# Two transformer-like blocks on one core: surplus tile spread over the last expert pack, combine and norms by token tile, second block's end reordered

## The chip, the cores and the metric

The kernel runs on one core of a Trainium2 chip. The metric is device time in microseconds of one launch, all weights read from HBM. The engines are TensorE (PE, with its weight loads as PEld), VectorE (DVE), ScalarE (ACT), GpSimd (POOL) and SyncE (SP, here the queue that issues nearly all transfers).

## What is computed

256 tokens of width 1024, in float32, pass through two blocks. Cut to what matters here:

```python
# end of the first block: hierarchical MoE, 32 experts, each token goes to 2 of them
h = h + sum_over_experts(combine[:, e] * (silu(xt @ w_gate[e]) * (xt @ w_up[e])) @ w_down[e])
x = rmsnorm(h, final_norm_g)                       # "first"
# second block
h = rms_norm(x, g_mix)                             # "mix2"
z = h @ w_in + b_in                                # 56 chunks of 128 columns
va, ga, xb, gb, sa, sb = split(z)
u = silu(layer_norm(causal_conv31(va * sigmoid(ga)), ln_g, ln_b));  y_a = u @ w_a_out
v = rg_lru(causal_conv4(xb));                      y_b = (v * gelu(gb)) @ w_b_out
x = x + (sigmoid(sa) * y_a + sigmoid(sb) * y_b) @ w_o
h = rms_norm(x, g_mlp)                             # "mlp2"
x = x + square(relu(h @ w_1)) @ w_2
return rms_norm(x, g_final)                        # "last"
```

An expert has a tile of 32 token slots. An expert with more tokens than that needs a surplus tile; `n_extra` counts them at run time, and with these inputs there is one.

## The kernel before, in words

All five engines run hand-written programs that meet at counting semaphores; each engine works strictly in program order. Dense products are float32 made of three faster passes: a matrix is kept as a rounded part ("hi", written by ScalarE) and the remainder ("rest", subtracted on VectorE or GpSimd), and `three_passes` (L1595 to L1597) multiplies hi by hi, hi by rest and rest by hi.

**Experts.** SP streams 6 MB for each expert (gate, up, down). `load_pair` (L465, L468) alternates two sets of three 2 MB slots: an expert's gate and up may be issued when the expert two before has finished its gate and up products (`gu_done`), its down when that one has finished down (`down_done`). Experts go in packs of four. Packs 1 to 6 are a loop, pack 7 is written out: TensorE does `expert_gate_up` (L1749) and `expert_down` (turn of the hidden rows L1756, products L1762) for experts 28 to 31, with the surplus tile between them under `pe.If(n_extra > 0)`: after expert 28's down come `over_gate_up(0)` (gather L1845, turn L1848, products L1749), then expert 29's gate and up, `over_down(0)`, expert 29's down, and `over_combine(0)` (L1868), which waits until VectorE has added the four results (L1355). Then come experts 30 and 31. `combine_pack` (L1775) multiplies the pack's weighted rows back to tokens in four parts, both token tiles of the first half of the columns and then both of the second; VectorE adds each to `X` (`add_pack`, L1247).

**Two norms.** After the last add, `moe_done` is set. VectorE writes HG = X * g_first (L1382), ScalarE sums the squares of X (L660) and of HG (L843); the root of the first norm and its reciprocal scale the sums for the second root (L1386, L1387, L848), then VectorE writes the normalised rows `HN` (L1391) and the new X (L1393). TensorE turns HN (L1588), VectorE applies the gain (L1031), ScalarE writes HT_hi (L676), VectorE HT_rest (L1040).

**In-projection.** 28 halves of 256 columns (1 MB each), in the order IN2_ORDER, four raw buffers in the slots that the experts' gate and up had. SP issues the first four after `down_done` of expert 30, later ones as buffers come free. ScalarE rounds each (`split_half`, L803), GpSimd subtracts (L600), except halves 16 to 18 and 22 to 25, which VectorE subtracts (L1403). TensorE makes two chunks from a half (`times_hT`), ScalarE takes them (L865). ScalarE's order is: take half n, then `split_half(n + 4)`. VectorE runs beside this: four pairs of the 31-tap convolution (L1411, L1418, L1425), six of the short one, the recurrence (L1462 to L1490) with one `rest_half` after each of its four groups.

**Layer norm.** Mean and variance over channels are products with a matrix of 1/1024 (`mean_ones`): `means()` (L1936) has 8 matmuls after the in-projection, `variances()` (L1942) 8 more after the third of the y_b products. **Out-projection.** Four halves of w_o, each for both token tiles (`o_ps`), then VectorE adds (L1547), the norm "mlp2" (L660, L663, L1016), turn, gain, hi, rest. `residual_first` (L1807) loads X into the four result banks by products with the identity. **MLP.** Two rounds of four w_1 blocks and four w_2 blocks of 2 MB. ScalarE rounds each (`split_mlp`, L963), VectorE subtracts (L1539). Inside a w_1 block ScalarE does four relus (L980), then `split_mlp` of a block four further on, then FT_hi (L983). **End.** When all of w_2 is used, VectorE copies four banks to X (L1573), ScalarE sums squares of both token tiles, one root, then L1576 writes the result, and SP stores it in two transfers (L553).

## Time and profile before

| | us |
|---|---|
| median of 3 runs | 1159.42 |
| lowest, highest | 1159.11, 1169.11 |
| the profiled execution | 1171.32 |
| its span on the core | 1169.5 |
| mean granted TensorE clock in it (1.0 is 2.4 GHz) | 0.891 |

The page gives for the span: PE busy 919.2 us (79%), PEld 745.3 (64%), DVE 497.5 (43%), ACT 369.0 (32%), POOL 203.5 (17%); 298 MB are read at a mean of 256 GB/s. Stamps below are microseconds from the start of the span. "Idle before <- X" is time in which the engine waited and what came last.

### The profile page before, as it was taken

The page shows a single profiled execution, that of the slowest core. Times are in us where ns is not written, and L with a number is a line of the kernel's source. Part 1 is how long each engine was busy: PE and PEld are TensorE (multiplying, and loading weights), DVE is VectorE, ACT ScalarE, POOL GpSimd, SP SyncE. Part 2 cuts the span into 40 slices and gives each one's busy share as a digit, 9 for nine tenths or more (in the row PEclk, how much of TensorE's full clock was granted, in tenths as well). Part 3 has the DMA queues.
Part 4 walks back from the last instruction along what each step waited for, and adds up shares of the span by engine and source line. Part 5 has one row for each costly group of instructions (what it writes and reads, how often), then busy time and mean ns, then how long its engine had stood idle before and what let it go on. Part 6 is the DMA issues. An engine that isn't in the chain of part 4 may idle for free.

```text
span 1169.5 us, 18121 instructions
## 1 busy us (share of the span) xinstructions
PE 919.2 (79%) x7868; PEld 745.3 (64%) x7868; DVE 497.5 (43%) x784; ACT 369.0 (32%) x508; POOL 203.5 (17%) x76
## 2 busy tenths in 40 slices
PE   4988486856666665657588489998999989999996
PEld 4977476524233333333254389778999988888985
DVE  5434623411212120202021649999973446453541
ACT  4452411110101010101011434456656443534330
POOL 1031400000000000000000688702139820000000
PEclk9997585977889787978797889999999998999998
DMA  9850370999999999999998445424556643354510
GB/s 356 256 220 1 128 304 1 392 421 421 424 422 424 421 421 421 422 421 421 422 421 370 146 149 179 144 73 144 167 173 235 217 148 140 145 215 163 197 72 36
DMA packets 94891, 299.79 MB, mean 256 GB/s; under 512 B 9165, under 2 KB 45565, under 8 KB 86653
## 3 DMA queue, kind: packets, MB, share of 16 engines
q1 hardware_dynamic: 94125, 297.95, 65.7%
q0 software_dynamic: 576, 1.18, 0.4%
q8 instruction: 34, 0.56, 0.2%
q14 instruction: 12, 0.10, 0.0%
q10 hardware_dynamic: 144, 0.00, 0.0%
HBM read 298.07 MB, written 1.05 MB: 256 GB/s over the span
## 4 chain that ended last, share of the span: by engine, by line
PE 53%; DMA 25%; DVE 14%; ACT 4%; issue 2%; SPq 1%; POOL 0%; DVEq 0%; ACTq 0%; POOLq 0%
DMA mem<-in_w_up 22%; PE PS L1595 12%; PE PS L1596 11%; PE PS L1597 11%; PE PS L1749 9%; DVE PS L1425 6%; PE PS L1762 3%; DMA mem<-in_w 2%; PE PS L1588 1%; PE PS L1737 1%; ACT mlp_hi L963 1%; DVE ring_rest L1403 1%; ACT mem L660 1%; DVE HN L1125 1%; DVE mem L1382 1%
## 5 line engine op out<-in xcount | busy, mean ns | idle before, releaser
L1749 PE MATMUL PS<-mem 128*32 128x256 f32 x2048 | 156.1, 472 | 111.4 <-DMA mem<-in_w_up 110.1
L1597 PE MATMUL PS<-HT_hi,ring_rest 128*128 128x256 f32 x768 | 218.8, 285 | 0.0
L600 POOL TENSOR_TENSOR ring_rest<-mem,z_hi 128x2048 fp32r<-128x2048 f32 x21 | 98.4, 4691 | 619.1 <-ACT z_hi L803 540.6
L1749 PEld LDWEIGHTS PS<-mem 128*32 128x32 f32 x2048 | 83.8, 135 | 185.0 <-issue 163.5
L1597 PEld LDWEIGHTS PS<-HT_hi,ring_rest 128*128 128x128 f32 x768 | 148.6, 193 | 0.0
L1595 PE MATMUL PS<-HT_hi,z_hi 128*128 128x256 f32 x448 | 129.2, 288 | 9.9 <-ACT mem L865 5.7
L1596 PE MATMUL PS<-HT_rest,z_hi 128*128 128x256 f32 x448 | 128.4, 287 | 0.0
L1234 DVE TENSOR_TENSOR mem<-mem,PS 128x128 f32<-128x128 f32 x32 | 9.2, 287 | 241.9 <-ACT mem L776 241.9
L1539 DVE TENSOR_TENSOR ring_rest<-mem,mlp_hi 128x4096 fp32r<-128x4096 f32 x16 | 70.6, 4425 | 82.4 <-ACT mlp_hi L963 82.4
L1595 PEld LDWEIGHTS PS<-HT_hi,z_hi 128*128 128x128 f32 x448 | 87.7, 196 | 11.9 <-ACT mem L865 6.1
L1425 DVE SCALAR_TENSOR_TENSOR PS<-mem,CAW,PS 128x256 f32<-128x256 f32 x232 | 91.2, 479 | 0.0
L1596 PEld LDWEIGHTS PS<-HT_rest,z_hi 128*128 128x128 f32 x448 | 87.6, 196 | 0.0
L776 ACT ACTIVATE mem<-PS 128x128 f32<-128x128 f32 x32 | 8.9, 278 | 239.8 <-PE PS L1749 239.8
L963 ACT ACTIVATE mlp_hi<-mem 128x4096 fp32r<-128x4096 f32 x16 | 57.8, 3624 | 81.6 <-DMA mem<-in_w 81.6
L1595 PE MATMUL PS<-HT_hi,mlp_hi 128*128 128x256 f32 x256 | 72.5, 283 | 4.2 <-ACT mem L980 4.2
L803 ACT ACTIVATE z_hi<-mem 128x2048 fp32r<-128x2048 f32 x28 | 53.5, 1914 | 68.2 <-DMA mem<-in_w_in 68.2
L1762 PE MATMUL PS<-mem 128*32 128x256 f32 x1024 | 63.0, 386 | 14.7 <-ACT mem L780 14.7
L1596 PE MATMUL PS<-HT_rest,mlp_hi 128*128 128x256 f32 x256 | 72.2, 282 | 0.0
L1239 DVE COPY mem<-PS 32x256 f32<-32x256 f32 x64 | 27.2, 424 | 71.5 <-PE PS L1762 70.8
L1762 PEld LDWEIGHTS PS<-mem 128*32 128x32 f32 x1024 | 36.5, 110 | 31.8 <-issue 20.6
L1588 PE MATMUL PS<-ident,HN 128*128 128x128 f32 x80 | 18.6, 424 | 43.9 <-DVE HN L1016 19.4
L1595 PEld LDWEIGHTS PS<-HT_hi,mlp_hi 128*128 128x128 f32 x256 | 48.6, 190 | 5.5 <-ACT mem L980 5.0
(322 smaller groups left out, 1887.7 us busy)
## 6 DMA issues: line engine op xcount, KB each, us to landing
mem<-in_w_gate SPq DMA_DIRECT2D x32, 2048.0 KB, 15.2
mem<-in_w_up SPq DMA_DIRECT2D x32, 2048.0 KB, 19.7
mem<-in_w_down SPq DMA_DIRECT2D x32, 2048.0 KB, 12.0
mem<-in_w SPq DMA_DIRECT2D x16, 2048.0 KB, 7.9
mem<-in_w_in SPq DMA_DIRECT2D x28, 1024.0 KB, 5.3
mem<-in_w_in SPq DMA_DIRECT2D x5, 2048.0 KB, 19.3
mem<-in_w_b_out SPq DMA_DIRECT2D x4, 1536.0 KB, 8.7
mem<-in_w_out SPq DMA_DIRECT2D x2, 2048.0 KB, 15.0
```

The costliest lines, as they stand in the source:

```text
L600: nc.gpsimd.tensor_tensor(z_rest(n), z_raw(n), z_hi(n).bitcast(F32), ALU.subtract).then_inc(z_rest_ready, 1)
L803: nc.scalar.activation(z_hi(n), z_raw(n), ACT.Copy).then_inc(z_hi_ready, 1)
L963: nc.scalar.activation(mlp_hi[n % 4][:, :], slot[late_slot[n % 4]], ACT.Copy).then_inc(mlp_hi_ready, 1)
L1239: ins = nc.vector.tensor_copy(Y[SLOTS * i:SLOTS * (i + 1), D_STRIP * j:D_STRIP * (j + 1)], PS[SLOTS * j:SLOTS * (j + 1), B_DOWN + i % 2, 0 ...
L1425: nc.vector.scalar_tensor_tensor(to, UP[:, ch, k:k + T], CAW[:, k * KC + ch:k * KC + ch + 1], acc[:, i, :], ALU.mult, ALU.add).then_inc(ta ...
L1539: nc.vector.tensor_tensor(ring_rest[late_slot[n % 4]][:, :], slot[late_slot[n % 4]], mlp_hi[n % 4][:, :].bitcast(F32), ALU.subtract).then_ ...
L1588: ins = nc.tensor.transpose(PS[:, 4 + n, k * P:(k + 1) * P], HN[:, tt, 4 * half + k, :], ident[:, :])
L1595: nc.tensor.matmul(dst, s_hi, m_hi, start=start and n == 0, stop=False, skip_group_check=True)
L1596: nc.tensor.matmul(dst, s_hi, m_rest, start=False, stop=False, skip_group_check=True)
L1597: ins = nc.tensor.matmul(dst, s_rest, m_hi, start=False, stop=stop and n == len(terms) - 1, skip_group_check=True)
L1749: ins = nc.tensor.matmul(PS[SLOTS * j:SLOTS * (j + 1), bank, 0:2 * F_STRIP].rearrange("p (w n) -> p w n", w=2), xg[:, k, :], w[:, :, k, F_ ...
L1762: ins = nc.tensor.matmul(PS[SLOTS * j:SLOTS * (j + 1), bank, 0:D_STRIP], hT[:, SLOTS * k:SLOTS * (k + 1)], w[:, k, D_STRIP * j:D_STRIP * ( ...
```

## The change

1. **Surplus tile.** Its parts move. TensorE: gather after expert 28's gate and up, gate and up after expert 29's, down after expert 29's down, combine after expert 30's gate and up; the wait for its adds moves to before expert 31's down. ScalarE's and VectorE's programs are cut accordingly. Surplus tiles from the second on, of which there are none here, come before expert 30's down.
2. **First loads of the in-projection** wait for the gate and up of expert 30 (not its down).
3. **Last combine by token tile**: both halves of tile 0, then of tile 1. Squares of a tile start when its own adds are done. `moe_done` goes.
4. **One root for both norms.** The second root takes the sum of squares of HG and, as bias, (eps/D * sum of squares of X + eps*eps), so that it waits for no first root; one root for each token tile. The first norm's own root and the new X come later (after HT_rest). GpSimd subtracts half 0 in four pieces and then waits for HG; half 1 goes to VectorE, ahead of the first convolution.
5. **First product in another order**: hi by hi and rest by hi for all k, and only then the passes that need HT_rest, also for the MLP. The first of the in-projection's rounds is written out.
6. **Layer norm**: VectorE sums the 8 chunks first (`tensor_reduce` of 2048 elements over a view with k innermost), so that one matmul stands in place of 8, for the mean and for the variance. The mean's goes before the last round of the in-projection; centring moves ahead of h_rest and the squares to half 25 in ScalarE's program.
7. **Out-projection** in the order WO_ORDER. X is turned as it is, unnormalised, by token tile (`turn_x3`), tile 0 before the last two steps. The norm of the MLP is applied at the end as the square of the reciprocal root (relu, squared, scales so). `residual_first` goes; the end does X = PSUM * r2 + X.
8. **MLP**: ScalarE does `split_mlp` after the second relu of the next block; both rounds are written out. The last w_2 block goes by result bank, token tile 0 first, and the end is done by token tile and half, with three stores.

```diff
-            sp.wait_ge(down_done, EXPERTS - 1)
+            sp.wait_ge(gu_done, EXPERTS - 1)
             for n in range(RAW):
                 load_z(n)
...
+            pool.wait_ge(z_hi_ready, 1)
+            for part in range(4):
+                at = slice(part * BLOCK, (part + 1) * BLOCK)
+                ins = nc.gpsimd.tensor_tensor(z_rest(0)[:, at], z_raw(0)[:, at], z_hi(0)[:, at].bitcast(F32), ALU.subtract)
+            ins.then_inc(z_rest_ready, 1)
+            pool.wait_ge(gained, TT)
...
+            pool.wait_ge(z_rest_ready, 2)
             for n in range(2, IN2_HALVES):
...
+            split_half(0)
             act.preload_act_table_set(SQRT_SET)
+            for tt in range(TT):
+                act.wait_ge(comb_free, 4 * (PACKS - 1) + 2 + 2 * tt + 2)
+                nc.scalar.activation(turned_rows[:, tt, :], X[:, tt, :], ACT.Square,
+                                     accum_out=ss[:, 10 + tt:11 + tt]).then_inc(first_squares, 1)
             for tt in range(TT):
                 act.wait_ge(gained, tt + 1)
+                link(nc.scalar.activation(square, HG[:, tt, :], ACT.Square, accum_out=ss[:, 12 + tt:13 + tt]))
+                if tt == 0:
+                    act.wait_ge(mix2_in, 1)
+                nc.scalar.activation(rstd[:, 12 + tt:13 + tt], ss[:, 12 + tt:13 + tt], ACT.Sqrt, scale=1.0 / D,
+                                     bias=ss[:, 8 + tt:9 + tt]).then_inc(rms_ready, 1)
+            rms("first", 10, TT, D)
+            split_half(1)
             split_half(2)
             split_hT("mix2")
             split_half(3)
...
+                if n == ACT_CENTRED:
+                    act.wait_ge(centred, 1)
+                    nc.scalar.activation(Z[:, Z_GA:Z_GA + KC, :], CU, ACT.Square).then_inc(sq_ready, 1)
...
                     for i in range(4):
                         act.wait_ge(f_ps, 4 * at + i + 1)
                         nc.scalar.activation(FT[:, 4 * b + i, :], PS[:, 4 + i, 0:T], ACT.Relu).then_inc(f_bank_free, 1)
-                    split_mlp(8 * half_n + b + 4)
+                        if i == 1 and b > 0:
+                            split_mlp(8 * half_n + b + 3)
...
             for tt in range(TT):
+                dve.wait_ge(comb_free, 4 * (PACKS - 1) + 2 + 2 * tt + 2)
                 nc.vector.tensor_tensor(HG[:, tt, :], X[:, tt, :], g_first[:, :], ALU.mult).then_inc(gained, 1)
+            dve.wait_ge(first_squares, TT)
+            nc.vector.tensor_scalar(ss[:, 8:10], ss[:, 10:12], EPS / D, EPS * EPS, ALU.mult, ALU.add).then_inc(mix2_in, 1)
             for tt in range(TT):
+                dve.wait_ge(rms_ready, rms_order.index("mix2") + tt + 1)
+                link(nc.vector.reciprocal(rstd[:, 12 + tt:13 + tt], rstd[:, 12 + tt:13 + tt]))
                 nc.vector.tensor_scalar(permuted(tt), plain(HG[:, tt, :]), rstd[:, 12 + tt:13 + tt], None, ALU.mult).then_inc(rows, 1)
...
             rest_hT("mix2")
+            inverse_rms("first", 10, TT)
+            for tt in range(TT):
+                nc.vector.tensor_scalar(X[:, tt, :], HG[:, tt, :], rstd[:, 10 + tt:11 + tt], None, ALU.mult)
...
+            rest_half(1)
             conv_a(0)
...
+            nc.vector.tensor_reduce(Z[:, Z_GA, :], CU.rearrange("p k t -> p t k"), AX_X, ALU.add).then_inc(sum_ready, 1)
...
                 rest_half(REST_SCAN[g])
+            dve.wait_ge(mean_ps, 1)
+            nc.vector.tensor_tensor(CU, CU, PS[:, 4, 0:T].unsqueeze(1).broadcast_to((P, KC, T)), ALU.subtract).then_inc(centred, 1)
...
+            add_out(0, 0)
+            add_out(1, 0)
             rest_mlp(0)
+            add_out(0, 1)
+            apply_gain("mlp2", G_MLP2, range(2))
+            rest_hT("mlp2", range(2))
+            add_out(1, 1)
+            apply_gain("mlp2", G_MLP2, range(2, 4))
...
             expert_gate_up(PACKS - 1, 0)
+            with pe.If(n_extra > 0):
+                over_gather(0)
             expert_down(PACKS - 1, 0)
+            expert_gate_up(PACKS - 1, 1)
             with pe.If(n_extra > 0):
                 over_gate_up(0)
+            expert_down(PACKS - 1, 1)
             with pe.If(n_extra > 0):
                 over_down(0)
+            expert_gate_up(PACKS - 1, 2)
             with pe.If(n_extra > 0):
                 over_combine(0)
...
+            expert_down(PACKS - 1, 2)
+            expert_gate_up(PACKS - 1, 3)
+            with pe.If(n_extra > 0):
+                pe.wait_ge(over_finished, 1)
+            expert_down(PACKS - 1, 3)
+            combine_pack(PACKS - 1, EXPERTS)
...
+            def turn_x3(tt):
+                pe.wait_ge(x3_ready, TT + tt + 1)
+                for half in range(2):
+                    for k in range(4):
+                        ins = nc.tensor.transpose(PS[:, 4 + 2 * tt + half, k * P:(k + 1) * P],
+                                                  X[:, tt, :].rearrange("p (q k) -> p k q", k=KC)[:, 4 * half + k, :], ident[:, :])
+                    ins.then_inc(turned, 1)
+
+            for step, (tt, n) in enumerate(WO_ORDER):
+                if step == WO_TURN:
+                    turn_x3(0)
...
+                    if half == 1 and b == 3:
+                        for n in (0, 2, 1, 3):
+                            for k in range(4):
+                                ins = w2_term(b, k, n, hi, rest, False)
+                            ins.then_inc(w2_last, 1)
```

WO_ORDER is ((0, 0), (1, 0), (0, 1), (1, 1), (0, 2), (0, 3), (1, 2), (1, 3)), each (token tile, half of w_o); WO_TURN is 6 and ACT_CENTRED 25.

## Rows read from the trace of the kernel before

**Rows 1.** Busy time by stage: stretch, its length, each engine's busy us, clock, transfers

```profile
150.00:652.00 502.00, 337.82 (x3766) 205.75 (x3765) 99.47 (x254) 67.30 (x162) 0.00 (x0) 0.83 0.93 383
652.00:677.00 25.00, 7.74 (x25) 4.76 (x26) 20.40 (x24) 16.83 (x21) 22.63 (x15) 0.68 0.40 118
677.00:874.00 197.00, 189.00 (x1456) 175.47 (x1456) 174.55 (x354) 101.58 (x142) 89.92 (x22) 0.98 0.45 147
975.00:1159.60 184.60, 180.37 (x1147) 162.68 (x1146) 80.16 (x31) 65.31 (x55) 0.00 (x0) 1.00 0.37 137
```

**Rows 2.** TensorE's timeline, 555 to 690: start, us, operation, [idle before, releaser]

```profile
634.65 6.46 PE L1749 MATMUL PS<-mem 128*32 128x256 f32 x64 [1.18 <-DVEq L1357]
...
644.33 3.66 PE L1749 MATMUL PS<-mem 128*32 128x256 f32 x64
...
649.49 1.93 PE L1762 MATMUL PS<-mem 128*32 128x256 f32 x32 [0.46 <-ACT mem L780]
652.45 3.86 PE L1775 MATMUL PS<-mem 128*128 128x512 f32 x8 [1.03 <-ACT mem L785]
669.23 3.67 PE L1588 MATMUL PS<-ident,HN 128*128 128x128 f32 x16 [12.93 <-DVE HN L1391]
676.79 0.57 PE L1595 MATMUL PS<-HT_hi,z_hi 128*128 128x256 f32 x1 [3.89 <-DVE HT_rest L1040]
```

**Rows 3.** SP's timeline, 560 to 720: issues of transfers

```profile
621.65 0.43 SPq L465 DMA_DIRECT2D mem<-in_w_up  x1
629.20 0.38 SPq L468 DMA_DIRECT2D mem<-in_w_down  x1
```

**Rows 4.** Transfers issued in 620 to 640: count, KB each, median us to landing

```profile
mem<-in_w_up SPq DMA_DIRECT2D x1, 2048.0 KB, 15.4
mem<-in_w_down SPq DMA_DIRECT2D x1, 2048.0 KB, 12.9
```

**Rows 5.** GpSimd's timeline, 560 to 720

```profile
654.25 9.97 POOL L600 TENSOR_TENSOR ring_rest<-mem,z_hi 128x2048 fp32r<-128x2048 f32 x2 [519.49 <-ACT z_hi L803]
```

**Rows 6.** Line L1382 alone: shortest, median, longest ns; first and last start

```profile
L1382 DVE TENSOR_TENSOR mem<-X,g_first x2: 2469/3994/5520, 657.4 to 659.8; 128x1024 f32<-128x1024 f32 x2
```

**Rows 7.** Groups by form, VectorE: busy us, mean ns of one, idle before

```profile
L1562 DVE TENSOR_TENSOR mem<-mem 128x1024 f32<-128x1024 f32 x8 | 9.8, 1219 | 2.1 <-ACT mem L980 2.1
...
L1280 DVE TENSOR_REDUCE extra_row<-mem 1x16 f32<-1x512 f32 x1 | 0.7, 674 | 0.0
...
L1174 DVE TENSOR_REDUCE mem<-mem 128x16 f32<-128x64 f32 x1 | 0.3, 265 | 0.0
```

**Rows 8.** VectorE's timeline, 690 to 965

```profile
692.88 0.69 DVE L1411 TENSOR_TENSOR mem<-mem,PS 128x512 f32<-128x512 f32 x1 [16.44 <-ACT mem L865]
...
835.90 2.28 DVE L1403 TENSOR_TENSOR ring_rest<-mem,z_hi 128x2048 fp32r<-128x2048 f32 x1
...
854.20 2.29 DVE L1403 TENSOR_TENSOR ring_rest<-mem,z_hi 128x2048 fp32r<-128x2048 f32 x1
```

**Rows 9.** Groups by form, TensorE, the mean and variance products

```profile
L1936 PE MATMUL PS<-mem,mean_ones 128*128 128x256 f32 x16 | 3.7, 386 | 0.6 <-ACT mem L865 0.6
L1942 PE MATMUL PS<-mem,mean_ones 128*128 128x256 f32 x16 | 3.6, 379 | 0.0
```

**Rows 10.** TensorE's timeline, 957 to 1000

```profile
966.67 3.67 PE L1588 MATMUL PS<-ident,HN 128*128 128x128 f32 x16 [3.97 <-DVE HN L1016]
...
974.06 0.45 PE L1595 MATMUL PS<-HT_hi,mlp_hi 128*128 128x256 f32 x1
```

**Rows 11.** TensorE's waits, 960 to 1169: total, times, longest

```profile
PE PS L1595 <- ACT mem L980: 4.2, 4, 2.7
```

**Rows 12.** The page's transfers: KB each, median us to landing

```profile
mem<-in_w SPq DMA_DIRECT2D x16, 2048.0 KB, 7.9
```

**Rows 13.** VectorE's timeline, 1159 to 1169

```profile
1159.57 2.48 DVE L1573 COPY X<-PS 128x512 f32<-128x512 f32 x4 [27.24 <-PE PS L1597]
...
1163.86 2.48 DVE L1576 SCALAR_TENSOR_TENSOR mem<-X,rstd,g_last 128x1024 f32<-128x1024 f32 x2
```

311 lines of the change are left out of this document (167 added, 144 removed).

## The prediction

> **What bounds the kernel now.** I read the stages first [rows 1]. From 150 to 652 us the transfers carry 383 GB/s at a busy share of 0.93 and TensorE is busy for 338 of 502 us: the weights bound the experts, and nothing in this change makes that stream shorter. From 652 to 677 nothing is full: TensorE works 7.7 of 25 us. From 677 on TensorE is busy for 189 of 197 us and, after 975, for 180 of 185: there time goes only with its work or its waits. So the change can gain in seams: after the last weight, before the first in-projection product, at the layer norm, between out-projection and MLP, and at the end. Then I read each seam in the timeline of its engine.
>
> **A, the experts' end.** Expert 31's up weights are issued at 621.65 and take 15.4 us, so they are there at 637.1; its down is issued at 629.20, takes 12.9 and is there at 642.1 [rows 3, 4]. Yet its gate and up products start only at 644.33 and its down products end at 649.49 + 1.97 = 651.5, because the surplus tile and the wait for its adds push expert 30's gate and up to 634.65 [rows 2]. With the parts spread, the same TensorE work (none is removed) ends expert 30 at about 634: its gate and up come at 624 instead of 635, and the combine with its adds, 4.4 us, goes behind them. The queue stays fed, as each issue still comes before the previous transfers are through, so the landings stay at 637 and 642. Expert 31's gate and up take 3.66 to 6.46 us by the clock [rows 2]: they end between 640.8 and 643.5, turn and hidden rows need 1.5 us (648.0 to 649.49), the down weights arrive at 642.1, and down takes 1.97: the end D lies between 644.2 and 647.0. I take 645.2: 6.3 us gained, 4.5 to 7.3. If only the landing of the down weights counted it would be the upper end; below nothing it can hardly be, since both starts are bounded by landings.
>
> **B, from D to the first in-projection product.** Before it is 676.8 - 651.5 = 25.3 us [rows 2]. The combine ends at D+4.9, the last add at D+5.6, as before. Then HG: two instructions of 2.5 and 5.5 us [rows 6], where the same size takes 1.22 us elsewhere [rows 7]. GpSimd ran two subtractions of 5 us from 654.25 to 664.2 [rows 5], and the second HG ended 1.1 us after the last of them: VectorE waited for whole GpSimd instructions. That agrees with the Trainium skill (SBUF — State Buffer, "Who interferes with whom"): the pair of ports is locked for a full instruction. Now GpSimd has one half, in four pieces of 1.2 us, started at about D+2.8 (half 0 lands about 3 us after the down weights, ScalarE rounds it in 1.9) and done by D+8. HG ends between D+8 and D+11; I take D+9.5 where it was D+13.8.
> From there, ScalarE squares each HG (1.25), one root each (0.3), a reciprocal (0.2), and the rows of tile 0 and 1 (1.3 each): tile 1 is written at D+13.3. ScalarE rounds halves 1 and 2 (3.8 us) from D+12.1, then the four pieces of HT_hi (2.4): D+18.3. TensorE's 3.7 us of turns and VectorE's gains are done by D+16 and lie under that. The first product no longer needs HT_rest, before 3.9 us of waiting [rows 2]. So D+18.4 for D+25.3: 6.9 gained, 5 to 8.5. VectorE's new X writes (1.6) and half 1's subtraction (2.3) end at about D+23, before TensorE is through with half 0 at D+26.5; without that cover each us later costs one. GpSimd's memsets and its 12 transfer issues, 14 us, move with HG and end at D+24; half 2, which is behind them, is wanted at D+32. The first four loads are issued as expert 30's gate and up are done, some 3 us ahead of its down, behind down 31 in the queue; they cost nothing and give nothing but cover.
> Everything in the next stage hangs on that first product: VectorE waited 16.4 us for its first convolution, until 692.88 [rows 8], 16.1 after the first product, through the fifth half's transfer, and that chain moves as one.
>
> **C, layer norm.** Removed: 3.7 + 3.6 us of products [rows 9]; added: two matmuls of two records, about 0.8 together. Added on VectorE: two sums of 2048 elements. The trace has no such one. Contiguous, 512 elements take 0.674 [rows 7], so 2048 some 2.2 to 2.7; over a strided view 64 take 0.265, which with a fixed part of 0.16 (1024 elements in 1.22 and 2048 in 2.28 [rows 7, 8]) is 1.7 ns an element, or 3.5 us. I take 2.8, between them. The first lies on the path: VectorE is busy without a gap before the scans and its four subtractions, the first from 835.90 and the last from 854.20 [rows 8], come every 6.1 us where TensorE needs 5.8 for a half, so TensorE is held by VectorE there. The last half then ends 2.8 later. The mean's products go (3.7), but w_b's subtraction on VectorE and the h remainders, behind the centring now, are late by about 3 and leave next to nothing: 0. The second sum lies under the y_b products, when VectorE waits anyway; the variance gives 3.0. C is 3.0, between 0 and 5.
>
> **D, out-projection to MLP.** Before: the last w_o product ends at 962.7, the first MLP product starts at 974.06: 11.4 us, with 3.97 of waiting for the norm, 3.67 of turns, and the rest, 3.7, in loading X by the identity [rows 10]. After: an add (0.85) and 8 turns (1.83) inside the stage, an add and 8 turns behind it, then gain and hi (1.5): 6.9. The squares and the root have left the path: ScalarE does them under the first block. 4.5 gained, between 0.8 and 5. The turns now read X with a step of 8 elements; no row shows TensorE reading so. If they took twice as long, the price is 3.7, and that is the lower end.
>
> **E, MLP.** TensorE waits 4.2 us for relus, 2.7 at once [rows 11]: ScalarE stands in `split_mlp`, waiting for a transfer, with relus behind it. Such a transfer takes 7.9 us [rows 12] and its rounding 3.6; a w_1 block takes 11.5. With two relus ahead, the other two come about 13 us after the block's start, and their banks are wanted 5.8 us into the next block, at 17. The wait after the four splits between the rounds (about 0.4) stays: 3.7 gained, 2 to 4.2.
>
> **F, the end.** From the last product to the last result there are 2.5 us of copies, 3.8 of squares, root and reciprocal, and the second of two 1.24 us products: from 1159.57 to 1166.4 [rows 13], 6.8 us. After: one add of half a tile (0.7), squares of it (0.85), root and reciprocal (0.6), with tile 0's two results between, then two half results: 3.8. Three stores in place of two are issued beside. 3.0 gained, 2 to 3.8.
>
> **Sum.** 6.3 + 6.9 + 3.0 + 4.5 + 3.7 + 3.0 = 27.4 us. The profiled execution took 1171.3 and would take 1143.9; the median of the runs is 1159.4, 12 us below it, and since no term scales with that difference I subtract from the median: 1132.0.
>
> **The rivals.**
> Strided reads are dear. For it: 0.265 us for 64 strided elements [rows 7]. Against: it is a single small row. The sums cost 3.5 (0.7 more on the path) and turns double (3.7): 23.0 gained, 1136.4. The Trainium skill says so (SBUF — State Buffer, "Door 1: The DMA port swizzle"): SBUF has lines of 16 bytes and each access that crosses to a new one pays; it gives no price for TensorE.
> The stream sets the end after all: if later issues (expert 30's down waits for the gather, 4 us more) leave the queue empty, expert 31's weights land as late as they are used now, A is 0: 21.1 gained, 1138.3. Against: 5 us of transfers stand ahead of each.
> The early start is lost in the in-projection. For: VectorE is busy 174.6 of 197 us there [rows 1] and gets more work. If its convolutions don't start earlier, A and B fall away and C to F stay: 14.2, 1145.2. Against: the 16.4 us that it waits.
> TensorE's clock, for slower than before: where it has gaps it runs at a mean of 0.83, in the dense stages at 0.98 [rows 1], and a gate and up took 6.46 us at the low level and 3.66 at the high one [rows 2]. The place is the first in-projection round, now written out and started out of order. If it stayed at 1.2 GHz, each us there would cost half a us; 55 us at the low level eat the gain, 78 make the kernel 1% slower, and 90 give 1132 + 45 = 1177. Against: the stage as it is now has a mean of 0.98, with its start in it.
> The change does nothing that is seen, as seams only move: 1159.
>
> **How the numbers follow.** Forecast 0.60, with 1125 to 1140 of its own (the terms' ends don't fall together); strided reads 0.13; stream 0.09; early start lost 0.12; clock 0.03; nothing 0.03. A measurement of this kernel can tell about 1%, 11.6 us, so faster is below 1147.8: the first three whole and most of the fourth, 0.90; the rest of it and nothing 0.07; slower 0.03. The range is 1122 to 1146: it takes in the strided and stream cases and the middle of the lost start.
>
> **What would show it.** Expert 31's down products end 2 to 4 us after its down weights land; each HG takes under 3.5 us; the first in-projection product comes 17 to 20 us after that end and the first convolution about 16 after it; the four scan-time subtractions still 6.1 apart and the sum before them 2.2 to 3.5; no mean or variance products of 3 us; turns of 8 at 1.8 us and 7 us between out-projection and MLP in all; no wait of over 1 us for relus; under 4 us from last product to last result. The prediction is wrong if the stage from 677 grows by more than the sum's 2.8 us, if turns take over 3 us, or if the down weights land after 645.

## The result, and the profile after the change

Over nine runs of each kernel the changed one has a median of 1153.28 us (1143.29 to 1155.56) and the one before 1167.81 us (1159.11 to 1170.56); the ratio is 0.9869, with a 95% interval of 0.9834 to 0.9905. So the change makes the kernel some 1.3% faster, 14.5 us by the medians, where 27.4 were forecast, and 1132.0 us, with a range that ended at 1146, was too low. Runs of both kernels fall into two groups some 10 us apart (1159 and 1166 to 1171 before, 1143 to 1145 and 1153 to 1156 after), for which I have no cause. Over all the profiles below, pack 6's combine, up to which the change touches nothing, starts anywhere between 585.2 and 596.1 us. Between single profiles I therefore count from the start of that combine.

The profiled execution took 1153.28 us (span 1151.5), that of before 1171.32 (1169.5). From pack 6's combine to the end of the span it is 558.1 us, before it was 574.1: 16.0 us less, and here is where they lie. D, as in the prediction, is the moment when expert 31's down products end. The other boundaries are first and last starts from the timelines; "product" is a TensorE product. The letters name the stretches as well.

```
stretch                                   before   after   gained  forecast
A  pack 6's combine to D                   56.03   54.49     1.54     6.3
B  D to first in-projection product        25.37   19.31     6.06     6.9
C  that to first product of w_a           238.62  238.26     0.36     3.0
   (of it, to the first product of w_b    201.29  203.78    -2.49)
   products of w_a                         22.51   22.51     0
D  first product of w_o to first of MLP    36.15   35.62     0.53     4.5
E  MLP, first to last product             185.08  180.80     4.28     3.7
F  last product to the end                 10.38    7.16     3.22     3.0
```

B, E and F are as forecast within 0.9 us, and their differences cancel. A, C and D are missing 4.8, 2.6 and 4.0 us: those 11.4 are the whole difference between 16.0 and the sum of 27.4.

**A.** TensorE's timeline of the kernel after the change, 624 to 652 us (start, us, operation, what ended the idle time before it); it answers to [rows 2].

```profile
626.74 3.88 PE L1928 MATMUL PS<-HT 32*128 32x512 f32 x8
635.55 0.48 PE L1819 MATMUL PS<-ident,mem 128*128 128x128 f32 x1 [4.94 <-issue]
636.49 3.64 PE L1825 MATMUL PS<-mem 128*32 128x256 f32 x32 [0.46 <-ACT mem L789]
639.88 4.56 PE L1812 MATMUL PS<-mem 128*32 128x256 f32 x64
...
645.94 1.93 PE L1825 MATMUL PS<-mem 128*32 128x256 f32 x32 [0.46 <-ACT mem L789]
```

The spread works: the surplus tile's combine (L1928) stands between expert 30's gate and up and its turn, and ends at 630.6. Then TensorE does nothing for 4.94 us, and the releaser is not an engine or a transfer but "issue". In the code that place holds one thing, `pe.If(n_extra > 1)` (L1946), the block for a second and further surplus tiles, which is never entered with this input. Before, the block stood behind the last combine, where TensorE waited 12.93 us for the rows HN anyway [rows 2]. Expert 31's down products end at D = 647.87, which is 54.5 us after pack 6's combine; the 645.2 of the forecast are 49.8 after it.

**B.** VectorE's timeline, 635 to 665 us. Each HG takes 2.2 us ([rows 6] have 2.5 and 5.5).

```profile
653.40 4.31 DVE L1429 TENSOR_TENSOR mem<-X,g_first 128x1024 f32<-128x1024 f32 x2
...
658.41 2.31 DVE L1435 TENSOR_SCALAR HN<-mem,rstd 128x1024 f32<-128x1024 f32 x1
660.57 0.16 DVE L1434 RECIPROCAL rstd<-rstd 128x1 f32<-128x1 f32 x1
660.79 2.83 DVE L1435 TENSOR_SCALAR HN<-mem,rstd 128x1024 f32<-128x1024 f32 x1
```

GpSimd's timeline, 640 to 665 us, the answer to [rows 5]:

```profile
650.70 5.93 POOL L612 TENSOR_TENSOR ring_rest<-mem,z_hi 128x512 fp32r<-128x512 f32 x4 [518.49 <-ACT z_hi L812]
657.78 2.02 POOL L615 MEMSET mem<- 128x2304 f32 x1 [1.15 <-DVE mem L1429]
659.85 2.83 POOL L616 MEMSET mem<- 128x2304 f32 x1
```

The four pieces are done by 656.6, D+8.8, and the second HG by D+9.8, where I had D+9.5. But the memsets that moved with them now run beside VectorE's rows HN, and those take 2.31 and 2.83 us where I had 1.3 each. The first in-projection product comes 19.3 us after D.

**C.** VectorE's timeline, 815 to 885 us ([rows 8] are the kernel before):

```profile
822.86 3.85 DVE L1521 TENSOR_REDUCE mem<-mem 128x256 f32<-128x2048 f32 x1
...
830.52 2.28 DVE L1447 TENSOR_TENSOR ring_rest<-mem,z_hi 128x2048 fp32r<-128x2048 f32 x1
...
848.83 2.28 DVE L1447 TENSOR_TENSOR ring_rest<-mem,z_hi 128x2048 fp32r<-128x2048 f32 x1
...
870.74 3.90 DVE L1548 TENSOR_REDUCE masks<-mem 128x256 f32<-128x2048 f32 x1
```

TensorE's waits, 655 to 890 us (what waited for what: total, times, longest):

```profile
PE PS L1658 <- DVE ring_rest L1447: 3.8, 1, 3.8
...
PE PS L1658 <- DVE ring_rest L1546: 1.3, 1, 1.3
```

The sums take 3.85 and 3.90 us. The four subtractions are 6.1 apart, the first 163.3 us after the first in-projection product where it was 159.1, and TensorE waits 3.8 us for one of them, a wait that it did not have; then 1.3 for w_b's. Behind the 3.8 us the granted clock is at its lower level for another 3 us (0.61 from 832 to 836 us), which no run prices by itself.

**D.** VectorE's timeline, 911 to 935 us, around the gates:

```profile
912.09 4.47 DVE L1579 TENSOR_TENSOR mem<-mem 128x512 f32<-128x512 f32 x1
...
917.62 3.96 DVE L1579 TENSOR_TENSOR mem<-mem 128x512 f32<-128x512 f32 x1
921.50 5.14 DVE L1568 TENSOR_TENSOR m_rest<-mem,m_hi 128x512 fp32r<-128x512 f32 x1
926.56 0.68 DVE L1578 TENSOR_TENSOR mem<-mem,PS 128x512 f32<-128x512 f32 x1
927.27 4.33 DVE L1579 TENSOR_TENSOR mem<-mem 128x512 f32<-128x512 f32 x1
931.53 0.68 DVE L1568 TENSOR_TENSOR m_rest<-mem,m_hi 128x512 fp32r<-128x512 f32 x1
```

GpSimd's timeline, 850 to 960 us:

```profile
873.17 22.50 POOL L645 TENSOR_TENSOR ring_rest<-mem,wb_hi 128x3072 fp32r<-128x3072 f32 x3 [11.97 <-ACT wb_hi L931]
895.61 20.40 POOL L645 TENSOR_TENSOR ring_rest<-mem,wa_hi 128x2048 fp32r<-128x2048 f32 x4
915.97 15.09 POOL L645 TENSOR_TENSOR ring_rest<-mem,wo_hi 128x2048 fp32r<-128x2048 f32 x3
```

L1579 is the second instruction of a gate, an addition, and L1568 writes `m_rest`, the remainder that the out-projection multiplies. L1568 takes 0.68 us when GpSimd is idle and 5.14 when it is not: with both inputs in SBUF, VectorE waits until GpSimd's instruction is over. GpSimd is busy without a gap from 873.17 to 931.06. Before the change it stood idle for 3.7 us at 904 and 3.1 us at 932, and of VectorE's additions and subtractions for the gates only one addition was held (4.84 us). The third gate's products are done by about 922.5 (each pair is 5.55 us behind the last), but it starts at 926.56, and TensorE waits for `m_rest`. Its own timeline, 927 to 955 us:

```profile
932.26 0.58 PE L1658 MATMUL PS<-wo_hi,m_hi 128*128 128x256 f32 x1 [3.44 <-DVE m_rest L1568]
932.64 0.41 PE L1659 MATMUL PS<-ring_rest,m_hi 128*128 128x256 f32 x1
932.86 0.41 PE L1660 MATMUL PS<-wo_hi,m_rest 128*128 128x256 f32 x1
...
953.03 1.16 PE L2042 MATMUL PS<-ident,X 128*128 128x128 f32 x8 [0.78 <-DVE X L1592]
```

Behind the wait the matmuls start every 0.21 us, where they started every 0.12. The windows say why (stretch, length, busy us of TensorE, its weight load, VectorE, ScalarE and GpSimd, clock, transfers):

```profile
930.90:934.90 4.00, 2.36 (x9) 2.07 (x10) 3.87 (x6) 1.96 (x3) 0.16 (x1) 0.62 1.05 401
934.90:938.90 4.00, 4.00 (x22) 4.00 (x21) 0.02 (x1) 3.97 (x3) 2.83 (x1) 0.53 0.10 36
938.90:942.90 4.00, 4.00 (x36) 4.00 (x35) 0.00 (x0) 4.00 (x2) 1.78 (x1) 1.00 0.00 0
```

The granted clock is at its lower level, 1.2 GHz, until about 938.7: 22 matmuls where the next window has 36. The strided turns themselves (L2042) are no part of it: eight take 1.16 us, 0.14 each.

**E and F.** TensorE's waits from 960 to the end: where [rows 11] have 4.2 us for relus, there is now this.

```profile
PE PS L1658 <- ACT mem L1007: 0.8, 1, 0.8
```

These 3.4 us are most of E's 4.28; where the other 0.9 lie I did not find. And VectorE's timeline from 1130 us, the last addition and the two last results:

```profile
1144.79 0.75 DVE L1631 SCALAR_TENSOR_TENSOR X<-PS,rstd,X 128x512 f32<-128x512 f32 x1 [1.97 <-PE PS L1660]
...
1147.17 1.41 DVE L1638 SCALAR_TENSOR_TENSOR mem<-X,rstd,g_last 128x512 f32<-128x512 f32 x2
```

Against [rows 13], where 6.8 us passed from the last product to the last result, it is now 1147.17 + 1.41 - 1144.79 = 3.8 us.

### The profile page after: what moved, and what is told of

Its sections match the earlier page's. It is cut to its first block, busy times and chain, and to the rows that moved or that the text cites. A ratio compares the mean times of both kernels' runs of the same rounds, so it can differ in the third digit from the quotient of the medians.

```text
span 1151.5 us, 18005 instructions
## 1 busy us (share of the span) xinstructions
PE 907.6 (79%) x7832; PEld 738.0 (64%) x7832; DVE 519.8 (45%) x788; ACT 371.5 (32%) x516; POOL 201.8 (18%) x78
## 3 DMA queue, kind: packets, MB, share of 16 engines
HBM read 298.07 MB, written 1.05 MB: 260 GB/s over the span
## 4 chain that ended last, share of the span: by engine, by line
PE 53%; DMA 25%; DVE 15%; ACT 3%; issue 3%; SPq 1%; DVEq 0%; ACTq 0%
DMA mem<-in_w_up 22%; PE PS L1658 12%; PE PS L1659 11%; PE PS L1660 11%; PE PS L1812 8%; DVE PS L1469 6%; PE PS L1825 4%; PE PS L1800 1%; PE PS L1651 1%; DVE ring_rest L1447 1%; DVE mem L1579 1%; DVE HN L1160 1%; DMA mem<-in_w 1%; PE PS L1838 1%; PE PS L1780 1%
## 5 line engine op out<-in xcount | busy, mean ns | idle before, releaser
L1660 PE MATMUL PS<-HT_hi,ring_rest 128*128 128x256 f32 x752 | 214.1, 285 | 0.0
L1660 PEld LDWEIGHTS PS<-HT_hi,ring_rest 128*128 128x128 f32 x752 | 145.2, 193 | 0.0
L1658 PE MATMUL PS<-HT_hi,z_hi 128*128 128x256 f32 x440 | 126.5, 287 | 9.6 <-ACT mem L891 5.8
L1659 PE MATMUL PS<-HT_rest,z_hi 128*128 128x256 f32 x440 | 125.9, 286 | 0.0
L607 POOL TENSOR_TENSOR ring_rest<-mem,z_hi 128x2048 fp32r<-128x2048 f32 x19 | 88.4, 4657 | 101.2 <-DVE ring_rest L1447 83.4
L612 POOL TENSOR_TENSOR ring_rest<-mem,z_hi 128x512 fp32r<-128x512 f32 x4 | 5.9, 1513 | 518.5 <-ACT z_hi L812 518.5
L1658 PE MATMUL PS<-HT_hi,mlp_hi 128*128 128x256 f32 x248 | 69.7, 281 | 0.8 <-ACT mem L1007 0.8
L1825 PEld LDWEIGHTS PS<-mem 128*32 128x32 f32 x1024 | 36.9, 113 | 34.1 <-issue 23.4
L1659 PE MATMUL PS<-ring_rest,FT_hi 128*128 128x512 f32 x128 | 50.4, 394 | 0.0
```

The costliest lines, as they stand in the source:

```text
L607: nc.gpsimd.tensor_tensor(z_rest(n), z_raw(n), z_hi(n).bitcast(F32), ALU.subtract).then_inc(z_rest_ready, 1)
L1658: nc.tensor.matmul(dst, s_hi, m_hi, start=start and n == 0, stop=False, skip_group_check=True)
L1659: nc.tensor.matmul(dst, s_hi, m_rest, start=False, stop=False, skip_group_check=True)
L1660: ins = nc.tensor.matmul(dst, s_rest, m_hi, start=False, stop=stop and n == len(terms) - 1, skip_group_check=True)
L1825: ins = nc.tensor.matmul(PS[SLOTS * j:SLOTS * (j + 1), bank, 0:D_STRIP], hT[:, SLOTS * k:SLOTS * (k + 1)], w[:, k, D_STRIP * j:D_STRIP * ( ...
```

## The experiments

Every kernel is the changed one with the edit shown. "Whole" is the time from pack 6's combine to the end of the span (558.1 in the changed kernel), A to F are the stretches of the table. Each of them comes from one profile. D, where the edit leaves it alone, is 34.1 to 35.9 us in five profiles, so that a difference of under 2 us between two of them says little.

**No block.** TensorE's never-entered block is removed (it would matter only with two or more surplus tiles).

```
-            with pe.If(n_extra > 1):
-                with pe.Fori(1, EXTRA_MAX) as j:
-                    with pe.If(j < n_extra):
-                        over_gather(j)
...
```

> Left out: TensorE's code for a second and later surplus tile (these inputs have one, so nothing that runs goes). Theory J (TensorE loses the 4.9 us behind the surplus tile's combine in jumping over that block): the wait before expert 30's turn falls under 1 us, expert 31's down products end 3 to 5 us earlier against the last common point (the combine of pack 6 to the end of expert 31's down: 54.5 us in the changed kernel, 50 to 51.5 here), and the whole is 3 to 5 us below the changed kernel. Rival W (it waited for ScalarE, VectorE or the surplus tile's adds): the wait stays at 4 to 5 us, the time is the same.

Whole 549.5, 8.6 less; A 48.90, 5.6 less. Of the other 3.0 us, 1.8 are in C and 1.5 in D (B gives 0.2 back). In D the clock is low for some 3 us behind an `m_rest` wait of 3.2, where the changed kernel has some 7 behind one of 3.4. Over four runs 1146.41 us (1140.48 to 1154.35), ratio to before 0.9811 (0.9731 to 0.9891). The issue wait is gone: the combine ends at 633.3 and the turn starts. Its timeline, 627 to 645 us:

```profile
629.43 3.88 PE L1928 MATMUL PS<-HT 32*128 32x512 f32 x8
633.25 0.33 PE L1819 MATMUL PS<-ident,mem 128*128 128x128 f32 x1
...
637.89 3.66 PE L1812 MATMUL PS<-mem 128*32 128x256 f32 x64 [0.28 <-DMA mem<-in_w_up]
...
643.07 1.94 PE L1825 MATMUL PS<-mem 128*32 128x256 f32 x32 [0.48 <-DMA mem<-in_w_down]
```

Now, and not before, both starts are ended by transfers. This is the state that step A forecast: D ends 1.9 us after its weights.

**Short block.** Is it any condition, or the length of what is jumped?

```
             with pe.If(n_extra > 1):
-                with pe.Fori(1, EXTRA_MAX) as j:
...
+                nc.tensor.matmul(PS[:, 0, 0:4], ident[:, :], ident[:, 0:4], start=True, stop=True)
```

> The changed kernel with the never-entered block on TensorE (for a second and further surplus tiles, two nested conditions and some 75 matmuls) replaced by a single condition over one matmul, at the same place. Theory (the stop of 4.9 us is the instructions behind a long jump being fetched, so it goes with the length of what is jumped): the issue wait falls to under 1 us and the time from pack 6's combine to the end of expert 31's down products is 49 to 50 us, as with no block at all (48.9), where it is 54.5 now. Rival (every condition that is not taken costs this): the wait stays at 4.5 to 5.5 us and the time at 54 to 55.

No issue wait, A 48.66, whole 549.4. A short block that is not taken costs nothing here; the long one, some 70 matmuls in a loop behind two conditions, costs 4.9 us. A row of the transfers agrees, of the changed kernel from 633.0 to 633.5, in the midst of the stop:

```profile
q8 instruction: 1, 0.02, 13.7%
```

The instruction queue moves a packet there; with the short block it moves none from 628 to 636. The Trainium skill has the mechanism (Runtime: NRT & Kernel Launch, "Instruction fetch mechanics"): a taken branch whose target is outside the fetched pages waits for a fetch. Here the stop was 4.8 to 5.5 us, over the six profiles that have it, beside a full weight stream. That the stop is this fetch is argued from the row and the length, not shown by itself.

**Block behind the last combine,** on TensorE, VectorE and ScalarE, with a semaphore for ScalarE; this keeps further surplus tiles computed.

```
                 over_combine(0)
+            expert_down(PACKS - 1, 2)
+            expert_gate_up(PACKS - 1, 3)
...
+            combine_pack(PACKS - 1, EXPERTS)
             with pe.If(n_extra > 1):
...
```

> Nothing left out: the block for later surplus tiles stands behind the last combine on TensorE, VectorE and ScalarE, as in the kernel before. Theory J: the jump then lies under TensorE's wait for the normalised rows (8.0 us in the changed kernel), so the gain is that of the kernel without the block: 50 to 51.5 us from pack 6's combine to the end of expert 31's down, and the first in-projection product again 19 to 20 us behind it. Rival: the jump costs VectorE or ScalarE, which are on the path there, 1 us or more, and half the gain goes.

A 51.83, 0.3 us above what was expected; 2.7 of it is a wait for expert 31's up weights, which land 42.9 us after pack 6's combine where they land at 41.7 without the block. B is 19.3 as before, whole 553.6, 4.6 less. TensorE waits there for VectorE's rows for 8 us anyway, so the jump is covered.

**Mean by eight matmuls,** without VectorE's first sum.

```
-            nc.vector.tensor_reduce(Z[:, Z_GA, :], CU.rearrange("p k t -> p t k"), AX_X, ALU.add).then_inc(sum_ready, 1)
+            dve.sem_inc(sum_ready, 1)
...
-            nc.tensor.matmul(PS[:, 4, 0:T], mean_ones[:, :], Z[:, Z_GA, :], start=True, stop=True).then_inc(mean_ps, 1)
+            for k in range(KC):
+                ins = nc.tensor.matmul(PS[:, 4, 0:T], mean_ones[:, :], CU[:, k, :], start=k == 0, stop=k == KC - 1)
```

> The mean alone goes back to 8 products of the centred chunks' sums on TensorE, ahead of the last round; VectorE's first sum (3.85 us) is gone. Theory S (that sum, on VectorE's unbroken chain before the scans, is what the stage lost): VectorE reaches its first subtraction between the scans 3.8 us earlier, TensorE's 3.8 us wait for it goes, and from the first in-projection product to ScalarE's last take of it there are 199 to 201 us (202.5 in the changed kernel, 197.4 before). Rival (the 8 products cost TensorE as much as the sum cost VectorE): 202 or more.

The 3.8 us wait is gone and the first subtraction comes 159.5 us after the first in-projection product, as before the change. ScalarE's last take of the stage starts 200.5 us after it, inside the expected 199 to 201. Yet the first w_b product is only 0.6 us earlier (203.2 against 203.8). Behind the sum stood another bound, in ScalarE's timeline of this run:

```profile
847.19 1.92 ACT L812 ACTIVATE z_hi<-mem 128x2048 fp32r<-128x2048 f32 x1 [3.94 <-DMA mem<-in_w_in]
...
864.25 2.77 ACT L931 ACTIVATE wb_hi<-mem 128x3072 fp32r<-128x3072 f32 x1 [1.68 <-DMA mem<-in_w_b_out]
```

ScalarE waits for the last in-projection half and for w_b. So the sum's own 3.85 us are mostly covered by transfers, and TensorE's wait for w_b's remainder becomes 2.7 us. The whole is 555.0, 3.2 less, and it comes from D: 31.9 us instead of 35.6. GpSimd has gaps again (1.40 and 1.05 us), two of the gates' additions take 1.97 and 1.46 us instead of 4.47 and 3.96, the longest `m_rest` wait is 1.6 us, and the clock stays up, as its window at the start of the out-projection shows:

```profile
931.80:935.80 4.00, 3.05 (x25) 2.83 (x25) 2.01 (x4) 3.20 (x3) 0.71 (x1) 1.00 1.05 403
```

This is D as forecast (36.2 - 4.5 = 31.7), at a full clock; in part by luck, as the waits for `m_rest` are 2.5 us in all where they were 1.3 before, and the turns are cheaper than I had them. Nor does the edit bring it reliably: with the same edit beside the later block (below), GpSimd has no such gaps, the wait is 2.3 us, the clock falls and D is 34.6.

**GpSimd in pieces:** its subtractions for w_a and w_o, four instructions for each.

```
...
+                for part in range(4):
+                    ks = slice(part * (KC // 4), (part + 1) * (KC // 4))
+                    ins = nc.gpsimd.tensor_tensor(rest[:, ks, :], raw[:, ks, :], hi.bitcast(F32)[:, ks, :], ALU.subtract)
...
```

> GpSimd's subtractions of w_a and w_o go in four pieces each. Theory P (VectorE's two-input instructions at the end of the y_a stage wait for whole GpSimd subtractions of 5 us, and TensorE for them): VectorE's adds at the gate (0.7 us alone; 4.5, 4.0 and 4.3 in the changed kernel) take under 2.2 us each, TensorE's wait before w_o falls from 3.7 to under 1.5 us, its slow stretch behind it goes, and from the last y_b product to the first MLP product it is 4 to 7 us less than 57.9. Rival (the queue of subtractions itself is late, not the lock): TensorE waits as long, for w_o's remainder in place of m's, and the time is the same.

Whole 557.5, only 0.6 less, so what was expected (4 to 7 us less between y_b and MLP, a wait under 1.5) did not come. The cure works at its place: the last gate comes 260.6 us after the first in-projection product instead of 264.9, and none of VectorE's gate instructions takes over 2.5 us. But TensorE still waits 2.7 us once for `m_rest`, the clock falls again, and falls once more behind a 1.7 us wait at the start of MLP, whose first 10 us run at a mean of 0.83 (E 182.4). The pieces also cost more in all: GpSimd's groups, 880 to 935 us (in the changed kernel eight whole ones take 40.1):

```profile
L650 POOL TENSOR_TENSOR ring_rest<-mem,wo_hi 128x512 fp32r<-128x512 f32 x16 | 23.2, 1488 | 0.0
L650 POOL TENSOR_TENSOR ring_rest<-mem,wa_hi 128x512 fp32r<-128x512 f32 x16 | 22.5, 1441 | 0.0
```

**Memsets later:** GpSimd's memsets wait for the rows HN.

```
             pool.wait_ge(gained, TT)
+            pool.wait_ge(rows, rows_before["mix2"] + TT)
```

> The changed kernel with GpSimd's memsets held back until VectorE has written the rows HN. Theory (GpSimd's memsets share the SBUF port with VectorE's row writes): each of the two row writes takes 1.3 to 1.5 us, as before the change, where it takes 2.31 and 2.83 now, and the first in-projection product comes 17.5 to 18.5 us after expert 31's down products, where it is 19.3. Rival (the rows are slow for their own sake, or ScalarE's copies set the first product anyway): the row writes stay above 2.2 us, or they fall and the first product stays at 19.3.

VectorE's timeline, 655 to 665 us:

```profile
660.88 1.35 DVE L1436 TENSOR_SCALAR HN<-mem,rstd 128x1024 f32<-128x1024 f32 x1
...
662.30 1.43 DVE L1436 TENSOR_SCALAR HN<-mem,rstd 128x1024 f32<-128x1024 f32 x1
```

The theory holds at its seam: 1.35 and 1.43 us, B 17.7. Nothing of it reaches the end: from D to the first w_b product it is 222.3 us, 0.8 less than in the changed kernel, and the whole is 558.8, in one run that has 1.3 us more in MLP, where the clock from 960 to 1000 is 0.96 and not 1.00. By this one run, what is won ahead of the in-projection is won only in part; differences of this size are within what single profiles differ by.

**Cover,** chunks 0 to 3 of the second out-projection product ahead of chunks 4 to 7 of the first.

```
+                    wo_terms(0, 0, range(4), 0)
+                    wo_terms(1, 0, range(4), 1)
+                    ins = wo_terms(0, 0, range(4, KC), 0)
...
```

> The changed kernel with the order of the first out-projection products changed: chunks 0 to 3 of the product (tile 0, block 0) are followed by chunks 0 to 3 of (tile 1, block 0) and only then by chunks 4 to 7, which need the last two m_rest; no work is added or taken away. Theory (the wait for m_rest costs its own length and then the low TensorE clock behind it): the wait falls from 3.4 to about 2 us; if the low clock follows any gap of this kind, the next 10 us still show matmuls of 0.21 us and the time from the fourth gate addition of the first four (57.85 us before the first MLP product now) falls by 1.4 only; if a gap of 2 us is too short for it, matmuls stay at 0.12 and it falls by 4 to 5 us. Rival (what follows is bound by VectorE or a transfer, not by TensorE): it stays within 0.5 of 57.85.

The wait stays 3.4 us: it stands ahead of chunks 2 and 3, which I had not seen, so the cover came behind it. D is still 1.9 us shorter (33.8): the second short wait is gone and the clock is back after 3 us instead of 6. But the clock is back as soon in the runs without the block and with the short one, which leave this stage alone (D 34.1 and 34.4), so that only some 0.5 us can be put down to the cover.

**Woven,** the same two products by pairs of chunks, so that twelve matmuls stand ahead of the wait instead of six.

```
+            for pair in range(KC // 2):
+                pe.wait_ge(out_rest_ready, 2 + pair + 1)
+                for tt in range(TT):
+                    ins = wo_terms(tt, 0, range(2 * pair, 2 * pair + 2))
...
```

> The changed kernel with the first two out-projection products woven by pairs of chunks: chunks 0 and 1 of (tile 0, block 0), then of (tile 1, block 0), then chunks 2 and 3 of both, and so on. So twelve matmuls instead of six stand ahead of the wait for the second m_rest. Theory (the wait costs its length, and one of over 2 us is followed by some 6 us of TensorE at 0.5 of its clock; one of 1.6 us was not, in the run with the mean by matmul): the wait falls from 3.4 to 2.7 us; the clock still falls but there is less work left in it, and the time from the first out-projection product to the first MLP product is 32.5 to 34.5 us, where it is 35.7 now, 33.8 with chunks 0 to 3 of the second product moved and 31.9 without the clock's fall. Rival (the clock's fall is chance from run to run): 35 us or more, or 32 or less at a wait of 2.7.

The wait is 2.6 us, the clock falls behind it for 3 us, D is 33.0, whole 555.0, all as expected. Against the two runs named above, which have the same 3 us at the low clock, D is 1.2 to 1.4 us less: the shorter wait and the missing second one.

The theory behind both, that a wait of over 2 us is followed by the low clock, does not hold up over the other waits on record. With the two cures that come next, TensorE waits 3.0 us for w_b's remainder and the clock stays at 1.00 from 859 to 867 us:

```profile
PE PS L1660 <- DVE ring_rest L1548: 3.0, 1, 3.0
```

Nor did it fall behind the 2.7 us wait for relus before the change [rows 11], or a 2.3 us wait at 829 us without the block. Yet in that same run a wait of 2.0 us for ScalarE, at 814 us, was followed by 3 us at the lower level, and in the changed kernel the same wait of 2.0 was not. The length of the wait alone does not say whether the clock falls, nor for how long; what else does is open.

**Combinations.** Two cures (block later, mean by matmul); five (with pieces, memsets later, cover); four (block later, mean by matmul, memsets later, woven).

> The changed kernel with two cures at once: the never-entered block for further surplus tiles stands behind the last combine on TensorE, VectorE and ScalarE, and the layer norm's mean is made by eight matmuls without VectorE's sum (the variance keeps its sum). Alone they made the part from pack 6's combine to the end 4.6 and 3.2 us shorter. Theory (they lie in different stages and add up): 550.3 us from pack 6's combine to the end, 7.8 less than the changed kernel, so a ratio to the kernel before of 0.980 where the changed kernel has 0.987. Rival (the earlier in-projection is given back at the next seam, as the kernel's own early start was): less than 5 us.

> The changed kernel with five cures: further surplus tiles' block behind the last combine, the mean by eight matmuls, GpSimd's subtractions of w_a and w_o in four pieces each, GpSimd's memsets behind the rows HN, and chunks 0 to 3 of the second out-projection product ahead of chunks 4 to 7 of the first. Theory (each stands at its own seam): 4.6 + 3.2 + 0.6 + 1 + 1.4 to 4 = 11 to 13 us less than the changed kernel, 545 to 547 us from pack 6's combine to the end and a ratio to the kernel before of 0.976 to 0.978. Rival (VectorE and TensorE in the scan stage are full and take back what comes earlier): 550 us or more, no better than the two cures.

> The changed kernel with four cures: further surplus tiles' block behind the last combine, mean by eight matmuls, GpSimd's memsets behind the rows HN, and the first two out-projection products woven by pairs of chunks; GpSimd's subtractions stay whole. Theory (with cover the m_rest wait falls under 2 us and TensorE's clock stays at its upper level): 31.5 to 32.5 us from the first out-projection to the first MLP product, 17.7 from expert 31's down products to the first in-projection product, and 545.5 to 547.5 us from pack 6's combine to the end, where the two cures gave 551.3 and the five 548.1; ratio to the kernel before 0.975 to 0.978. Rival (what is won at these seams comes back as waits of VectorE): 549 us or more.

```
         runs  median us (range)             ratio to before (95%)     whole   A      D
two       4    1143.42 (1138.38 to 1148.87)  0.9807 (0.9747 to 0.9868)  551.3  48.65  34.6
five      6    1144.02 (1137.86 to 1150.84)  0.9812 (0.9763 to 0.9861)  548.1  48.57  32.7
four      6    1145.94 (1143.36 to 1147.15)  0.9809 (0.9780 to 0.9838)  549.6  49.05  30.4
```

All lie below the changed kernel's 0.9869 (0.9834 to 0.9905), though each interval overlaps that one, and the kernel without the block has 0.9811 by itself. None was better than another, and none reached the 0.975 to 0.978 that I had expected of the larger ones. So beyond the block the runs' times show no further gain; what the other cures do is seen in the profiles alone. In the four, TensorE's waits from 895 us show why D is 5.2 us shorter, and the window that the clock did not fall:

```profile
PE PS L1661 <- DVE m_rest L1571: 1.1, 2, 0.9
```

```profile
929.90:933.90 4.00, 3.76 (x31) 3.56 (x30) 1.99 (x4) 3.21 (x3) 0.72 (x1) 1.00 1.04 397
```

But the first w_b product came 205.9 us after the first in-projection product, 2.1 later than in the changed kernel, and the first convolution 19.0 us after it where it was 16.4: there the rival held. In the five, the first w_o product came 2.3 us late, and VectorE's timeline, 895 to 920 us, has the reason:

```profile
897.27 16.11 DVE L1588 TENSOR_TENSOR mem<-mem 128x512 f32<-128x512 f32 x1
913.30 0.68 DVE L1587 TENSOR_TENSOR mem<-mem,PS 128x512 f32<-128x512 f32 x1
914.01 0.69 DVE L1588 TENSOR_TENSOR mem<-mem 128x512 f32<-128x512 f32 x1
```

GpSimd's timeline of it, 880 to 940:

```profile
880.73 22.11 POOL L651 TENSOR_TENSOR ring_rest<-mem,wa_hi 128x512 fp32r<-128x512 f32 x16
902.78 10.05 POOL L651 TENSOR_TENSOR ring_rest<-mem,wo_hi 128x512 fp32r<-128x512 f32 x8
```

One addition of 128x512, 0.69 us by itself, took 16.11: GpSimd ran piece behind piece, and VectorE came in only when the queue was empty, at 912.8. So pieces don't by themselves let the other engine in between; in the run with pieces alone they did.

## Why the prediction was wrong, point by point

**A** failed in the step "the end D lies between 644.2 and 647.0. I take 645.2". Landings and TensorE's work were right, as the run without the block shows (7.1 us gained, between its bounds of 4.5 and 7.3). What I left out is the code between: I moved the parts but put the jump over the other surplus tiles' block at nothing. It stopped TensorE for 4.9 us and accounts for the missing 4.8. Before, such a jump stood under a 12.9 us wait [rows 2]. It is a cost that was moved out of its cover.

**B** was right in its mechanism (HG 4.3 us where it was 7.9, first product at D+19.3 where I had D+18.4). The term that was mis-sized is the rows: "the rows of tile 0 and 1 (1.3 each)" are 2.31 and 2.83, since "GpSimd's memsets ... move with HG" beside them. The run with later memsets gives 17.7.

**C** failed twice. "I take 2.8" for the first sum: it measured 3.85, above the 3.5 of the dear end; this view, with k innermost, costs VectorE about 1.9 ns an element (3.85 us / 2048). And "w_b's subtraction ... late by about 3 and leave next to nothing": it left a 1.3 us wait. The mean's products went, but the stretch to the first w_b product grew by 2.5 us, and the variance's share returned 2.9. The run with the mean by matmul says that a cheaper sum alone would not have brought the 3.0 either: the transfers of the last half and of w_b come next.

**D** failed at a place that no step names. Strided turns were cheap, 1.16 us for eight where I had 1.83 (from rows at the low clock), and from the last w_o product to the first of MLP it is 3.6 us, where add, turns, gain and hi came to 4.2 in my sum. But I counted from the last w_o product on and left w_o's start as it was. The wait for `m_rest` there grew from 1.3 to 3.7 us, because GpSimd's subtractions lost their gaps and held VectorE, and the low clock behind it cost the rest: against the run with the mean by matmul, 35.6 - 31.9 - (3.7 - 2.5) = 2.5 us. So the term left out is the wait for `m_rest` with the clock behind it, which I had at nothing; the four cures, with 1.1 us of it and a full clock, have D at 30.4. I had used this very exclusion in B, from [rows 5] and [rows 6], and not looked for it here. By the Trainium skill (SBUF — State Buffer, "Who interferes with whom") a VectorE instruction with two SBUF inputs contends with GpSimd's reads; the traces agree, 0.68 us against 5.14, and the gate that reads PSUM keeps its 0.68.

**E and F** held: 4.3 us (0.1 above its range) and 3.2 us for 3.7 and 3.0.

**The rivals.** The strided reads were dear on VectorE (1.05 us over the forecast) and not at all on TensorE. The stream did not set the end: only where TensorE did not stop at the block did transfers end its waits for expert 31, and without the block D came 7.1 us earlier. The early start was not lost in the in-projection: the first convolution comes 16.4 us after the first product, where it came 16.1. The stretch to the first w_b product is still 1.9 us longer than before even with the mean by matmul, and whether the early start has a part in this is not shown: in the three runs that change only the block, and so begin earlier still, the stretch was shorter. TensorE's clock cost time, but at the out-projection, some 2.5 us, not in the first round of the in-projection.

**The base.** The step "I subtract from the median" took 1159.42, the median of three runs (1159.11, 1159.42 and 1169.11); nine runs have 1167.81. That is 8.4 us of the 21.3 by which 1132.0 was too low. Of the other 12.9, 11.4 are A, C and D, and 1.5 is the difference between what the profiles gained from pack 6's combine on, 16.0, and the medians, 14.5. Profile against profile, 1171.32 - 27.4 = 1143.9 was forecast and 1153.28 came: with 2.0 us that were won ahead of pack 6's combine, the difference is the 11.4 us of A, C and D.

What stays open: without a long block at that place (none, short, or later) the first w_b product also comes 1.5 to 2 us sooner after the first in-projection product (202.3, 202.1 and 201.7 us against 203.8). 0.6 to 1.0 us of it is there from the first convolution on (15.8, 15.8 and 15.4 us after that product against 16.4); for the rest I have no cause, and the combinations, which have no long block there either, do not agree (204.2, 201.8 and 205.9).

## What to carry to other kernels

When work is moved, list what remains between its old neighbours as well: a block that is never entered is a jump, and this long one cost TensorE some 5 us where no wait covered it. When an engine loses its gaps, look at every instruction of the engine that shares its port, not only at the seam that the change is about. A wait of TensorE in the midst of dense work was followed here, in some places and not in others, by some 3 or 7 us at half its clock; by these rows it can cost 1.5 to 3.5 us (an estimate: half of that stretch) on top of its length, and its length alone does not tell whether it will. Matmuls that are put ahead of it shorten the wait. And a base from three runs can be 8 us off the median of nine.

## What was not expected of the hardware

The stop at a long block that is not taken: 4.94 us, 5.5 in one profile, none over a block of one matmul. VectorE held out for 16.11 us by a row of GpSimd instructions of 1.4 us each, far past a single one. TensorE's clock behind waits: for `m_rest` it fell after 3.4, 2.7, 2.6, 2.3 and 2.1 us and not after 1.6, 1.3 and 0.9, but elsewhere not after 3.0 and 2.7 us and yet after 2.0. TensorE turned X, read with a step of 8 fp32 elements, in 0.14 us each at the upper clock level; [rows 10] have 0.23 at the lower one, so the step cost next to nothing. VectorE's sum over a view with k innermost took 1.9 ns an element.
